# Normalised rows of a decoder layer's MLP read back in 32-element pieces and turned by VectorE in 32x32 blocks, in place of TensorE transposes

## The reference, cut to what matters

```python
x = layer_norm(DEEPNORM_ALPHA * x + g1 * mix, ln1_g, ln1_b)
h2 = x * (1.0 + sc2) + sh2
f = jnp.einsum("btf,fd->btd", jnp.square(jax.nn.relu(jnp.einsum("btd,df->btf", h2, w_up))), w_down)
x = layer_norm(DEEPNORM_ALPHA * x + g2 * f, ln2_g, ln2_b)
```

## Time and profile before

| | |
|---|---|
| Median of three runs | 2046.99 us |
| Profiled execution, its own time | 2046.98 us |
| Its span in the profile | 2045.2 us |
| PE busy | 2010.2 us (98%) |
| VectorE (DVE) busy | 1433.6 us (70%) |
| ScalarE (ACT) busy | 895.0 us (44%) |
| GpSimd (POOL) busy | 1457.0 us (71%) |
| Granted TensorE clock, mean | 0.997 |
| DMA over the span | 175 GB/s, packets under 512 bytes 12720 of 134046 |

### The profile page before, as it was taken

How to read it: one execution, slowest core, us unless ns; L and a number is a source line. 1 busy time by engine, 2 the same in 40 slices (tenths; PEclk the granted TensorE clock), 3 DMA queues, 4 the chain that set the end, 5 groups by cost and what they waited for, 6 DMA issues and landing times.

```text
span 2045.2 us, 27557 instructions
## 1 busy us (share of the span) xinstructions
PE 2010.2 (98%) x10278; PEld 1688.0 (83%) x10278; DVE 1433.6 (70%) x1866; ACT 895.0 (44%) x1242; POOL 1457.0 (71%) x1117
## 2 busy tenths in 40 slices
PE   7999999999999999999999999999999999999996
PEld 5678888888987888888888888888888899999995
DVE  3556697795857355587888576888757778775786
ACT  3223222222133654456555554665454655444442
POOL 4355898863433677788888788788788876666686
PEclk9999999999999999999999999999999999999998
DMA  9687888853433544545445545434654534454341
GB/s 348 250 269 237 250 276 245 289 175 129 147 95 97 184 139 163 189 141 174 134 145 186 206 162 167 155 125 153 217 186 144 175 109 140 144 183 147 123 146 47
DMA packets 134046, 357.48 MB, mean 175 GB/s; under 512 B 12720, under 2 KB 46425, under 8 KB 130841
## 3 DMA queue, kind: packets, MB, share of 16 engines
q1 hardware_dynamic: 133049, 352.58, 52.5%
q10 hardware_dynamic: 864, 3.15, 0.5%
HBM read 321.22 MB, written 34.44 MB: 174 GB/s over the span
## 4 chain that ended last, share of the span: by engine, by line
PE 74%; DVE 6%; ACT 0%; issue 0%; POOL 0%; DVEq 0%; ACTq 0%; POOLq 0%
PE ps L1237 24%; PE ps L1239 24%; PE ps L1238 24%; PE ps L1454 1%; PE ps L1525 1%; DVE htmp L1810 0%; DVE mix L1643 0%; DVE acc L1805 0%; DVE acc L1804 0%; DVE hid_a L1932 0%; DVE hid_b L1932 0%; PE ps L1315 0%; DVE mix L1642 0%; DVE spl L1643 0%; DVE pair_sums L1954 0%
## 5 line engine op out<-in xcount | busy, mean ns | idle before, releaser
L898 POOL TENSOR_TENSOR w_hilo<-w_raw,w_hilo 128x512 fp32r<-128x512 f32 x890 | 1280.8, 1469 | 548.5 <-ACT w_hilo L998 548.4
L998 ACT ACTIVATE w_hilo<-w_raw 128x1024 fp32r<-128x1024 f32 x445 | 470.3, 1058 | 519.6 <-PE ps L1239 415.8
L1237 PE MATMUL ps<-hA,w_hilo 128*128 128x512 f32 (+1 forms) x1760 | 619.9, 352 | 0.8 <-DVE acc L1839 0.8
L1239 PE MATMUL ps<-hA,w_hilo 128*128 128x512 f32 (+1 forms) x1760 | 618.3, 351 | 0.0
L1238 PE MATMUL ps<-hA,w_hilo 128*128 128x512 f32 (+1 forms) x1760 | 618.2, 351 | 0.0
L1237 PEld LDWEIGHTS ps<-hA,w_hilo 128*128 128x128 f32 x1760 | 330.2, 188 | 45.2 <-issue 2.2
L1238 PEld LDWEIGHTS ps<-hA,w_hilo 128*128 128x128 f32 x1760 | 330.3, 188 | 41.6
L1239 PEld LDWEIGHTS ps<-hA,w_hilo 128*128 128x128 f32 x1760 | 330.2, 188 | 41.2
L2040 DVE TENSOR_TENSOR acc<-acc,ps 128x512 f32<-128x512 f32 x270 | 177.8, 685 | 69.5 <-PE ps L1239 66.4
L1237 PE MATMUL ps<-w_hilo,hid_a 128*128 128x512 f32 x450 | 177.8, 395 | 0.3 <-ACT more_sums L1199 0.3
L1089 ACT ACTIVATE htmp<-ps 128x512 f32<-128x512 f32 x96 | 57.4, 598 | 273.9 <-PE ps L1239 266.7
(11 more groups left out here) (234 smaller groups left out, 2774.4 us busy)
## 6 DMA issues: line engine op xcount, KB each, us to landing
w_raw<-in_w_up SPq DMA_DIRECT2D x128, 512.0 KB, 3.5
w_raw<-w_mix SPq DMA_DIRECT2D x124, 512.0 KB, 3.2
w_raw<-in_w_down SPq DMA_DIRECT2D x97, 512.0 KB, 3.6
w_raw<-in_w_in SPq DMA_DIRECT2D x64, 512.0 KB, 4.8
xt<-in_w_ada SPq DMA_DIRECT2D x20, 1024.0 KB, 7.5
w_raw<-in_w_out SPq DMA_DIRECT2D x32, 512.0 KB, 4.5
xt<-x_norm SPq DMA_DIRECT2D x19, 512.0 KB, 5.3
xt<-in_w_down SPq DMA_DIRECT2D x36, 256.0 KB, 5.0
```

What stands on the lines that cost most here:

```text
L898: ins = pool.tensor_tensor(W[:, g % SLOTS, 1, cols], raw[:, g % RAW, cols], W[:, g % SLOTS, 0, cols], ALU.subtract)
L998: act.activation(W[:, g % SLOTS, 0, :], raw[:, g % RAW, :], ACT.Copy).then_inc(hi_done, 1)
L1237: pe.matmul(out, w_hi, x_hi, start=start, stop=False)
L1239: return pe.matmul(out, w_lo, x_hi, start=False, stop=stop)
```

## The change

`next_n` reads every tile of 256 features by 512 tokens with eight loads in place of one load of 128 tokens by 1024 features. A load fills 32 partitions: partition p takes, of each of 16 runs of 32 tokens, token p, and 32 features (128 bytes) of it. So a load has 512 pieces of 128 bytes and 64 KB, and a group's input takes 32 loads, 16 behind each of the two slabs. Each of the four tiles has a semaphore of its own. VectorE then turns 128x512 elements at once in blocks of 32x32 into the PSUM bank that TensorE wrote before (`n_turn`), eight times a group: tile 0 behind the sums of K4 of the seventh block, tile k + 1 just ahead of the split of tile k. TensorE's `n_transposes` and its calls go. ScalarE's part and the splits stay.

```diff
+BLK = 32
...
-        n_stage = sem("n_stage")
+        n_part = [sem(f"n_part{j}") for j in range(4)]
...
-                sp.dma_start(next_rows[t], n_rows(s + 1, t)).then_inc(n_stage, 16)
+                rows_of_group = x_norm[(s + 1) * GT:(s + 2) * GT, :].rearrange("(a p) f -> p a f", p=BLK)
+                for half in range(2):
+                    for c in range(P // BLK):
+                        f = 2 * P * t + P * half + BLK * c
+                        sp.dma_start(next_rows[t][BLK * c:BLK * c + BLK, GT * half:GT * half + GT].rearrange(
+                                         "p (a i) -> p a i", i=BLK),
+                                     rows_of_group[:, :, f:f + BLK]).then_inc(n_part[t], 16)
...
-            def n_transposes(s, k):
-
-                pe.wait_ge(n_stage, 64 * (s + 1))
-                if k >= 2:
-                    pe.wait_ge(x_split, KD * (SUPERS + s + 1) + k - 1)
-                elif s == 0:
-                    pe.wait_ge(h2s_split, 1)
-                for t in range(4):
-                    ins = pe.transpose(ps[:, 2 + k % 2, P * t:P * t + P], next_rows[t][:, P * k:P * k + P],
-                                       ident[:, :])
-                ins.then_inc(n_tr, 1)
-
...
-                k = feature_after(kind, b, i)
-                if k is not None:
-                    n_transposes(b // BLOCKS, k)
...
+            def n_turn(s, k):
+
+                dve.wait_ge(n_part[k // 2], 128 * (s + 1))
+                src = next_rows[k // 2][:, GT * (k % 2):GT * (k % 2) + GT]
+                signal(dve.transpose(ps[:, 2 + k % 2, :], src), n_tr, KD * s + k + 1)
...
                 k = feature_after(kind, b, i)
+                if (kind, i) == ("K", 4) and r == BLOCKS - 2 and s < SUPERS - 1:
+                    n_turn(s, 0)
                 if k is not None:
+                    if k < KD - 1:
+                        n_turn(s, k + 1)
                     n_feature(s, k)
```

## The result

The changed kernel takes 2064.5 us, the median of five runs (2064.08 to 2065.43), against 2046.99 for the kernel before in five runs beside it (2043.77 to 2047.81): a ratio of 1.0088, 95% interval 1.0077 to 1.0098. That is 17.5 us slower, inside the range and on the side that was forecast, but over twice the 8.3 us of the sum.

What follows compares the result with a forecast made beforehand. VectorE's chain of sums at three group ends was taken to bound the kernel: six turns add 4.32 us, 1.54 comes off, 2.78 each, loads at nothing; 2046.99 + 8.3 = 2055.3 us, range 2049 to 2072.

Steps and rivals of the forecast that it cites:

- the 8.3 us of the sum: Whole kernel: three group ends, each 2.78 us longer, add 8.3 us to 2046.99.
- The bound: First three group ends: VectorE's sums for the eighth block's fifth K slab delay the next group's first up-product by 2.78 us.
- TensorE's 3.86 us of transposes: Each group end: eight sets of four transposes cost TensorE 3.86 us, 0.48 a set; removed, they turn into waits.
- The turn: VectorE at group ends: one 128x512 turn takes 0.72 us; six in the chain add 4.32 us a stretch.
- The other sum: Whole kernel, alternative price: at the page's 311 ns per 128 columns a turn is 1.24 us, adding 17.7 us.
- The chain without the bursts: VectorE at the first group end: works from 949.15, starting the eighth block's fifth K slab's sums at 975.31.
- The issue time: SP's queue: each load in pieces takes 0.65 us to issue, so a burst of 16 holds SP 10.4 us.
- rival 1: Group ends: bursts outlast their cover and TensorE waits for slabs; 2079 us at 1.02 us a load; chance 0.20.
- So it is hidden with 1.0 us to spare: Behind each burst: the next slab is ready 1.0 us before TensorE wants it, so the loads cost nothing.
- Rival 3: Group ends: GpSimd, shifted, leaves three VectorE operations alone, saving 2.8 us of chain; 2041.7 us with cheap turns; chance 0.07.
- "Up to 1 us": Behind the stretch: VectorE's last sums come some 4 us later, priced at nothing; failing cover would cost up to 1 us.
- The pieces' data: DMA engines: a load's 512 pieces of 128 bytes take 0.49 to 1.52 us; low end taken, so issuing sets the pace.

Runs made afterwards that it cites:

- after_late_sums: The changed kernel with VectorE's combinations of a group's last block put off to behind later K slabs; 2054.95 us.
- early_turns_late_sums: The changed kernel with loads spread, turns done in place in SBUF in VectorE's idle time, and combinations of a group's last block put off; 2043.24 us.
- turns_only: The changed kernel with four plain loads per group in place of the 32 in pieces, turns kept on VectorE; 2057.9 us.
- pieces_only: The kernel before, TensorE's transposes kept, with the 32 loads in pieces per group in two bursts of 16; 2053.1 us.
- spread_loads: The changed kernel with the same 32 loads in pieces, four behind each of four slabs in place of 16 behind one; 2058.68 us.

## Why the prediction was right, and where it was wrong

- **The bound** was right. VectorE's chain to K'4's sums sets U'0, TensorE's 3.86 us of transposes turned into waits for VectorE's sums, and after_late_sums shows that taking work out of that chain shortens the stretch by nearly as much (4.1 and 3.92 us).
- **The turn** was right: 0.72 us, with 0.75 from one start to the next operation where the pitch of 0.72 was taken; six of them make 0.2 us of difference. The 3.86 us for TensorE's transposes hold too: in early_turns_late_sums, which has none, the stretch is 24.48 us and 1.5 for its one wait. The other sum that the prediction gives, 17.7 us, lies near the measured 17.5 by accident: it takes 1.24 us for a turn that took 0.72.
- **The chain without the bursts** was nearly right: 26.80 us in turns_only against 26.16. The turns' pitch is 0.2 of the 0.64, and the split of K6's stretch, 1.45 us where it took 0.99 before, most of the rest. The forecast's 8.3 us belongs beside the 11.1 of turns_only: of the 9.2 us that it was short, 2.8 stand there, some 2.0 of them in the three stretches, and 6.3 in pieces_only.
- **The issue time** was right in size: 0.56 us a load where 0.65 was taken. K5 did not wait, and rival 1 did not happen.
- **The step that failed** is "So it is hidden with 1.0 us to spare". It asked one question, whether the slab is ready when TensorE wants it, and that one it answered rightly. It did not ask when GpSimd would then work. The loads, priced at nothing, cost 6.3 us (pieces_only). The slabs were issued 5.92 us later against K5's start, and the margin that hid this was GpSimd's: its subtractions moved into the one gap in which VectorE's pair sums had been alone. In the first stretch the chain came out 28.64 us (979.38 - 950.74) against the 26.16 predicted, 2.48 more: the pair sums 3.01 (the differences to 0.43, 0.43, 0.42 and 1.45, with their pitch), less 1.04 given back by the split behind them (1.22 us for 2.26), plus 0.30 for K6's split, plus 0.2 for the turns, with the two combinations at -0.21 and +0.18. Another 0.3 lies ahead of and behind the chain.
- **Rival 3** had the right observation, that VectorE's operations between SBUF tiles come in two speeds by whether they meet GpSimd, and even named the shift against GpSimd as what decides. It looked only for operations that would gain by it. The first pair sum stands in the rows on the fast side, 0.43 us at 949.15, and GpSimd's timeline before shows three of the four there, so they had the most to lose. A shift should have been priced in both directions.
- **"Up to 1 us"** for the late sums behind the stretch, priced at nothing, stands beside 1.1 us more between the stretches (0.88 and 0.24). TensorE's waits there for ScalarE's step on these sums are 0.3 us in each, beside 0.3 in one of them before, so that most of the 1.1 us has no cause shown.
- **The pieces' data** were no cost that can be told. spread_loads shows it: as many pieces, and no more time than turns_only within their intervals. There are 50,496 more packets under 512 bytes (63216 - 12720), and the queue's share of its engines' span is 53.7%, where it was 52.5% before: 0.537 x 2063.7 - 0.525 x 2045.2 = 34.5 us more on each of 16 engines, an estimate of some 11 ns per small packet, net.

The third stretch of the changed kernel is shorter than the other two by the same rule. Its first pair sum takes 0.46 us, because it starts 0.18 us ahead of the end of a subtraction, and its first combination falls into a gap of GpSimd:

```profile
1625.09 0.46 DVE L1950 TENSOR_TENSOR pair_sums<-htmp 128x256 f32<-128x256 f32 x1 [5.54 <-ACT htmp L1108]
...
1643.61 1.23 DVE L2055 TENSOR_TENSOR more_sums<-more_sums,acc 128x1024 f32<-128x1024 f32 x1
```

In the second stretch these two take 1.25 and 2.34 us: 0.79 + 1.11 = 1.90, and the stretches differ by 1.89. What stays open is how such meetings fall in a kernel that has not been run; they hang on a few tenths of a microsecond between the two engines, and no run fixed that.

## What to carry to other kernels

When a change holds a queue back, it is not enough that the consumer on the critical path still gets its data in time: follow the delay through each engine in between, and see beside which instructions of the others it now works. An operation that runs at its fast speed only because another engine happens to be idle (here 0.42 us against 1.40) is a cost that is waiting to appear, so look for both speeds in the trace before; the most it can lose here is one instruction of the other engine. And work that is moved to a busier engine is best put where that engine waits: the same turns that cost 11.1 us in the chain gave 3.3 us when they stood in VectorE's idle time, with their loads spread.

## What was not expected of the hardware

TensorE's waits and clock in the changed kernel, first stretch. Its timeline at the K slabs that wait (the bracket is the idle time):

```profile
957.33 0.47 PE L1246 MATMUL ps<-w_hilo,hid_a 128*128 128x512 f32 x1 [2.61 <-DVE acc L2040]
...
965.28 0.47 PE L1246 MATMUL ps<-w_hilo,hid_a 128*128 128x512 f32 x1 [0.65 <-DVE acc L2040]
```

and its clock in stretches of 2 us (us, busy PE, PEld, DVE, ACT, POOL, clock, DMA share, GB/s):

```profile
955.00:957.00 2.00, 0.00 (x0) 0.00 (x0) 1.93 (x3) 0.51 (x1) 2.00 (x2) 1.00 0.47 99
957.00:959.00 2.00, 1.67 (x5) 1.38 (x6) 1.97 (x4) 1.97 (x4) 0.59 (x1) 0.70 0.66 212
959.00:961.00 2.00, 2.00 (x6) 1.52 (x6) 1.93 (x3) 1.97 (x4) 1.16 (x1) 0.50 0.56 221
961.00:963.00 2.00, 2.00 (x10) 1.66 (x9) 1.97 (x4) 1.56 (x2) 1.38 (x2) 0.95 0.00 0
```

TensorE did nothing in the 2 us up to 957, waiting for VectorE's first sums, and the granted clock behind it was 0.70, then 0.50, that is the lower of its two levels, 1.2 GHz in place of 2.4, and 0.95 of the full one from 961 on. The kernel before shows 1.00 over its whole stretch. It happened once in each of the three stretches (each has a mean of 0.95), behind waits of 2.61, 2.42 and 1.99 us, though not behind a wait of 1.99 us in the second. It cost nothing here that can be seen, since VectorE worked on without a gap and TensorE had to wait for it again at 965.28, 972.75 and 980.21; in a kernel that TensorE bounds it would not be free.

GpSimd itself was little slowed by meeting VectorE: ten subtractions in 13.24 us are 1.32 each, beside 1.26 in the block of eight at 937.02 before and 1.44 in that of fourteen at 950.29. Most of the loss fell on VectorE, whose first three pair sums took over three times as long; a subtraction that starts while a pair sum still runs takes 1.44 to 1.47 us in that block, the others 1.29 to 1.30.
